# Four weight sums in DRAM moved out of the attention into the first merge pieces of a two-block layer

## The chip, the cores and the metric

The kernel runs on one core of a Trainium2 chip. The metric is the device time of one execution in microseconds. TensorE (PE in the profile) multiplies; VectorE (DVE) and ScalarE (ACT) work element by element; GpSimd (POOL) does little arithmetic here and issues the accumulating DMAs; SyncE (SP) issues nearly all the others.

## The reference, cut to what matters

Two transformer-like blocks run over 256 tokens of width 2048, in float32. The part that the change touches is in the second block, its projection, attention and merge, and the weights of its feed-forward part:

```python
proj = h @ w_in[i]                        # (256 x 2048) @ (2048 x 9216): u, v_sgu, q, k, v_att, g_a, g_b
z = einsum('bhqd,bhkd->bhqk', qi, kf) * scale
log_beta = log_sigmoid(z)
log_1m = where(strict, log_sigmoid(-z), 0)
tail = cumsum(log_1m, reverse=True) - log_1m
w = where(strict, exp(log_beta + tail), 0)
y_b = einsum('bhqk,bhkd->bhqd', w, vf)
merged = sigmoid(g_a) * (y_a @ w_up_a) + sigmoid(g_b) * (y_b @ w_up_b)
x = x + merged @ w_o
hid = rmsnorm(x) @ w_ffn_in
x = x + (silu(gate) * up) @ w_ffn_out
```

## The kernel before, in words

**Pieces.** All weights go through TensorE in 848 pieces of 256 rows by 512 columns (512 KB), numbered by `g`. Each piece passes four stages. SP loads it into the ring `raw` (8 slots, one load of 1 MB for two pieces). ACT copies it to `whi` in the format fp32r (`split_hi`), DVE subtracts to get the rest, `wlo` (`split_lo`, line 1874), and TensorE multiplies: eight matmuls with `whi` (line 1357), then four with `wlo` (line 1362), 512 columns each. `whi` and `wlo` have four slots (`RING`), so ACT and DVE can be at most four pieces ahead. ACT waits for TensorE to be done with the slot's last piece; SP waits for DVE (`lo_ready`) to be done with the slots that it fills.

**Order of the stages.** A (pieces 0 to 127), C, DP and D are the first block. E1 (pieces 196 to 275) is the projection of the second one, ten slabs of eight pieces, E2 (from piece 276, `g_plan`) the merge, G the output projection, F the feed-forward part, J the last gate. In E1 the attention is woven between the pieces, `w` counting them from 196: its two halves `b` begin at `ATT_START` = 35 and 55, which is piece 231 and piece 251. At `w = z0 + 5` DVE takes the scores (`att_take`), at `z0 + 6` and 7 ACT does Abs, Exp and Ln, at `z0 + 9` DVE makes the logs (`att_logs`: `Lp`, its mask, then `zt`), at `z0 + 10` TensorE does the tail matmuls (`att_tail`, lines 1622 to 1624, 12 in all), at `z0 + 14` DVE subtracts them (`att_arg`), and so on. At piece 235 TensorE also transposes the last keys (`tr2_slab`, line 1336); their banks are those that `att_take` frees. Ten `form_step`s at the pieces `FORM_AT` make sums of activations for the merge. After slab 4 of E1 SP issues `held` and `held_p` (2 MB and 0.5 MB from SBUF to DRAM).

**The merge.** Three groups of columns of the merge, and nine of the feed-forward part, are computed by a scheme with seven instead of eight products (pieces "s", half as many columns of work each: six matmuls, lines 1722 and 1726). It needs sums of weight tiles. Some of these are made beforehand in DRAM, in `summed[i]`, four for each group, group `c` reading number `4c` to `4c + 3`: SP copies one 1 MB term to `summed[i]` (line 670, `copies_for_sums`), and GpSimd adds the other with an accumulating DMA (line 881, `add_in_dram`). `SUM_AT[i]` is the piece at which this happens: SP issues the copy in front of the load of that piece, so some eight pieces ahead, after waiting for sum `i - 4`; GpSimd issues the add when TensorE has reached that piece. Between the adds GpSimd computes reciprocal roots (`POWS`), and `SUMS_UPTO` says up to which piece the sums stand in front of each. After them come the adds into `r1` for the merge groups (line 896).

**The plan of the loads.** From piece 276 on the loads come from a list, `PLAN.loads`, of (piece whose split frees the slot, piece that needs it, kind, ...), sorted by the first two. For the first merge group it holds, in this order: pair 280 (free at 269), pair 282 (271), pair 276 (273), pair 278 (275), pair 284 (277), pair 286 (279), halves 295 (280) and 296 (281), `r1` for 290 and 292 (282, two loads of 1 MB), halves 297 (282) and 298 (283), pair 288 (285), pair 294 (287). The load of `r1` for group 0 (`load_r1`, line 766 on) also waits until TensorE has done the first six pieces from 276 on (line 769) and for `ya2_ready`. `copies_for_sums(need)` is called in front of each.

Of the kernel before, what the change touches and what calls it, by code (L numbers as in the profile page):

```python
# [87 lines left out]
M_GROUPS = len(MERGE_S)  # L88
# [34 lines left out]
class Plan:  # L123
# [129 lines left out]
    def plan_s_loads(self, groups):  # L253

        n = self.halves
        for c in groups:
            at = lambda i: self.s_at[(c, *S_ORDER[i])]
            for h in range(2):
                free = {0: self.g_plan + 6, M_GROUPS: self.g_block}.get(c)
                free = self.s_at[c - 1, "M4", 2 * h + 1] if free is None else free  # L260
                self.loads.append((free, self.s_at[c, "M1", 2 * h], "r1", h, c))
                self.loads.append((self.s_at[c, "M1", 2 * h + 1], self.s_at[c, "M5", 2 * h], "fifth", h, c))
            for i, (m, q) in enumerate(S_ORDER):
                for what, first, last in (("b21", "M2", "M2"), ("b22", "M6", "M3"), ("seventh", "M7", "M7")):
                    if m == first:
                        slot = RAW // 2 + n % 4
                        need = at(i - S_LEAD if m == "M6" else i)
                        self.loads.append((self.last_use[slot], need, "half", slot, (c, what, q)))
                        self.half[c, what, q] = (slot, 16 * (n // 4 + 1))
                        self.last_use[slot] = self.s_at[c, last, q]  # L270
                        n += 1
        self.halves = n
# [42 lines left out]
def two_blocks_kernel(nc, A, out):  # L315
    PLAN = Plan()
# [3 lines left out]
    with ctx:  # L320
# [142 lines left out]

        summed = nc.dram_tensor("summed", (4 * S_GROUPS, P, 4 * COLS), F32, kind="Internal").ap()
        SUM_AT = [int(24 + SUM_STEP * i) for i in range(int(116 // SUM_STEP) + 1)] + [144 + 8 * i for i in range(7)]
        SUM_AT += [199 + int(5.4 * i) for i in range(14)]
        SUM_AT += [PLAN.g_out + 11 + 6 * i for i in range(4 * S_GROUPS - len(SUM_AT))]

        acc = ctx.enter_context(nc.psum_tensor("acc", [P, 4, COLS], F32))
# [352 lines left out]
        @block.gpsimd  # L822
        def _(pool):
            made = [0]

            def link(ins):
                made[0] += 1
                ins.then_inc(sem("pool_step"), 1)

            def settle():  # L830
                pool.wait_ge(sem("pool_step"), made[0])

            link(pool.memset(ident[:, :], 0.0))
            settle()
            link(pool.affine_select(out=ident[:, :], in_=ident[:, :], compare_op=ALU.not_equal, fill=1.0, base=0,
                                    pattern=[[-1, P]], channel_multiplier=1))
            settle()
            pool.sem_inc(sem("ident_ready"), 1)
            link(pool.memset(ones[:, :], 1.0))
            link(pool.memset(lmask[:, :, :, :], 1.0))  # L840
            link(pool.memset(flip[:, :], 0.0))
            link(pool.memset(sel[:, :, :], 0.0))
            settle()

            link(pool.affine_select(out=causal[:, :], in_=ones[:, 0:P], compare_op=ALU.is_ge, fill=0.0, base=0,
                                    pattern=[[1, P]], channel_multiplier=-1))
            link(pool.affine_select(out=strict[:, :], in_=ones[:, 0:P], compare_op=ALU.is_gt, fill=0.0, base=0,
                                    pattern=[[1, P]], channel_multiplier=-1))
            link(pool.affine_select(out=later[:, :], in_=ones[:, 0:P], compare_op=ALU.is_gt, fill=0.0, base=0,
                                    pattern=[[-1, P]], channel_multiplier=1))  # L850

            link(pool.affine_select(out=sel[:, :, :], in_=sel[:, :, :], compare_op=ALU.not_equal, fill=1.0, base=0,
                                    pattern=[[-1, 4], [0, P]], channel_multiplier=1))

            link(pool.affine_select(out=flip[:, :], in_=flip[:, :], compare_op=ALU.not_equal, fill=1.0, base=-(P - 1),
                                    pattern=[[1, P]], channel_multiplier=1))

            for n, s in enumerate(LEVELS[1:]):
                for t, (first, sign) in enumerate(((0, 1), (P - 1, -1))):
                    m = lmask[:, n, t, :].rearrange("p (n s) -> p n s", s=s)  # L860
                    link(pool.affine_select(out=m, in_=m, compare_op=ALU.is_ge, fill=0.0, base=first,
                                            pattern=[[-2 * s, 64 // s], [0, s]], channel_multiplier=sign))
            settle()
            for n, s in enumerate(LEVELS[1:]):
                for t, (first, sign) in enumerate(((0, 1), (P - 1, -1))):
                    m = lmask[:, n, t, :].rearrange("p (n s) -> p n s", s=s)
                    link(pool.affine_select(out=m, in_=m, compare_op=ALU.is_ge, fill=0.0, base=s - 1 - first,
                                            pattern=[[2 * s, 64 // s], [0, s]], channel_multiplier=-sign))
            link(pool.memset(minus_half[:, :], -0.5))
            settle()  # L870
            pool.sem_inc(sem("consts_ready"), 1)
            added = [0]

            def add_in_dram(upto):

                while added[0] < upto:
                    i = added[0]
                    added[0] += 1
                    pool.wait_ge(piece_used, SUM_AT[i])
                    pool.wait_ge(sem(f"copied{i % 4}"), 16 * (i // 4 + 1))  # L880
                    pool.dma_start(summed[i], sum_terms(i)[1], accum_op=ALU.add, max_dma_last_dim=8192)\
                        .then_inc(sem(f"summed{i % 4}"), 16)

            for i, (name, n) in enumerate(POWS):
                add_in_dram(len([g for g in SUM_AT if g <= SUMS_UPTO.get(name, 0)]))
                if name == "qk0":

                    pool.wait_ge(sem("ws_loaded"), 16)
                    pool.affine_select(out=wsT[:, :, :], in_=wsT[:, :, :], compare_op=ALU.is_ge, fill=0.0, base=0,
                                       pattern=[[0, 8], [1, P]], channel_multiplier=-1).then_inc(sem("ws_masked"), 1)  # L890
                if name in ("ffn", "ple"):
                    for c in range(M_GROUPS) if name == "ffn" else range(M_GROUPS, S_GROUPS):
                        for m, (what, before) in S_DMA.items():
                            for q in range(4):
                                pool.wait_ge(lo_ready, S_AT[c, before, q] + 1)
                                pool.dma_start(r1[:, q], s_weights(c, what, q), accum_op=ALU.add).then_inc(sem(f"r1_added{q}"), 16)
                if name == "ffn":
                    add_in_dram(len(SUM_AT))
                pool.wait_ge(pow_in, i + 1)
                pool.tensor_tensor(rstd[:, i, 0:n], var[:, i, 0:n], minus_half[:, 0:n], ALU.pow).then_inc(pow_out, 1)  # L900
# [961 lines left out]
        def _(dve):  # L1862
# [523 lines left out]
            def strict_blocks(x):  # L2386
                d = diagonal_blocks(x)
                return dve.tensor_tensor(d, d, strict[:, :].unsqueeze(1).unsqueeze(1).to_broadcast([P, 4, 2, P]), ALU.mult)

            def att_logs(b):  # L2390

                dve.wait_ge(sem("att_ln"), b + 1)
                link(dve.scalar_tensor_tensor(out=Lp[:, :, :], in0=zt[:, :, :], scalar=0.0, in1=ab[:, :, :], op0=ALU.max, op1=ALU.add))
                strict_blocks(Lp).then_inc(sem("att_l"), 1)
                link(dve.scalar_tensor_tensor(out=zt[:, :, :], in0=zt[:, :, :], scalar=0.0, in1=ab[:, :, :], op0=ALU.min,
                                              op1=ALU.subtract))

# [43 lines left out]
                        link(ins)  # L2441
                ins.then_inc(sem("ya2_ready"), 1)

            FORM_AT = [46, 47, 48, 50, 52, 54, 57, 58, 61, 65]

            def form_step(i):

# [16 lines left out]
            for s in range(10):  # L2464
                n = FIRST["E1"] + s
                for p in range(8):
# [49 lines left out]
                    for b, z0 in enumerate(ATT_START):  # L2516
                        if w == z0 + 5:
                            att_take(b)
                        if w == z0 + 9:
                            att_logs(b)  # L2520
                        if w == z0 + 14:
                            att_arg(b)
                        if w == z0 + 18:
                            att_mask(b)
                        if w == z0 + 21:
                            att_output(b)
# [317 lines left out]
```

## Time and profile before

| | us |
|---|---|
| median of 3 runs | 1904.59 |
| lowest and highest of them | 1903.56 and 1905.67 |
| the profiled execution | 1904.34 |
| its span (first to last instruction) | 1902.6 |
| TensorE busy (matmuls) | 1881.0 |
| VectorE busy | 1473.6 |
| ScalarE busy | 1141.5 |
| GpSimd busy | 129.6 |

The 16 DMA engines moved 535.95 MB, 282 GB/s on the mean. Matmul records are pipelined: one of 512 columns lasts 379 ns in the profile, but the next starts 216 ns after it. "PEclk" is the clock that TensorE was granted, 1.00 for 2.4 GHz; 0.50 is 1.2 GHz. In brackets stands the idle time of the engine before an instruction, and what ended it. The names `raw`, `ple` and `in_w_ffn_in` in the rows cover more than one tensor of the same place.

### The profile page before, as it was taken

Reading aid. Unit: us, or ns where it says so; the run is one execution under the profiler, and the core shown is the slowest. Engines: PE = TensorE matmul, PEld = TensorE weight load, DVE = VectorE, ACT = ScalarE, POOL = GpSimd, SP = SyncE. Lnnn points to the kernel's source line nnn. Section 1 sums busy time; section 2 is a strip of 40 time slices with the busy share of each in tenths; the row PEclk is TensorE's granted clock in tenths of the full one; section 3 lists DMA queues with packets and bytes.
Section 4 is the critical chain, followed back from the end, with each engine's and each line's share of the span. In section 5 each row is a group of like instructions: output and inputs, shape, how many; then the busy total and the mean of one; then the engine's idle time right before and its main releaser. Section 6 shows DMA issues by size and latency. Waiting matters only on the chain.

```text
span 1902.6 us, 23371 instructions
## 1 busy us (share of the span) xinstructions
PE 1881.0 (99%) x9018; PEld 1645.4 (86%) x9018; DVE 1473.6 (77%) x1591; ACT 1141.5 (60%) x1417; POOL 129.6 (7%) x156
## 2 busy tenths in 40 slices
PE   9999999999999989999999999999999999999998
PEld 8888888888888878888888888888888888888887
DVE  6889776655666757769899657989898999898865
ACT  7556445555565545656776555666766676666553
POOL 4000001000001100100000000000000000000000
PEclk9999999999999999999999999999999999999999
DMA  9799898999889999857987886798879887987653
GB/s 390 266 285 311 265 309 275 341 342 347 288 280 323 339 317 297 267 214 244 317 286 245 342 265 223 262 320 277 268 260 329 273 269 260 332 249 250 218 192 131
DMA packets 86815, 535.95 MB, mean 282 GB/s; under 512 B 10416, under 2 KB 11184, under 8 KB 40752
## 3 DMA queue, kind: packets, MB, share of 16 engines
q1 hardware_dynamic: 72736, 458.69, 63.3%
q0 software_dynamic: 13824, 75.50, 20.5%
q8 instruction: 72, 1.18, 0.2%
q10 hardware_dynamic: 144, 0.26, 0.0%
q14 instruction: 39, 0.32, 0.0%
HBM read 529.69 MB, written 105.38 MB: 334 GB/s over the span
## 4 chain that ended last, share of the span: by engine, by line
PE 86%; DVE 5%; DMA 4%; issue 3%; ACT 2%; POOL 1%; ACTq 0%; DVEq 0%; POOLq 0%
PE acc L1357 40%; PE acc L1362 20%; PE aux L1722 13%; PE aux L1726 7%; DMA raw<-in_w_in 2%; DVE wlo L1874 1%; PE aux L1336 1%; DVE wlo L2549 1%; ACT whi L926 1%; PE aux L1429 1%; DMA ple<-in_w_in 1%; DMA ple<-in_w_ffn_in 0%; PE aux L1803 0%; DVE ple L2544 0%; POOL rstd L900 0%
## 5 line engine op out<-in xcount | busy, mean ns | idle before, releaser
L1874 DVE TENSOR_TENSOR wlo<-raw,whi 128x1024 fp32r<-128x1024 f32 x512 | 624.0, 1226 | 313.9 <-ACT whi L926 306.7
L926 ACT ACTIVATE whi<-raw 128x1024 fp32r<-128x1024 f32 x511 | 533.9, 1054 | 466.4 <-PE acc L1362 413.1
L1357 PE MATMUL acc<-whi,actA_hi 128*128 128x512 f32 x892 | 344.1, 386 | 0.6 <-ACT whi L926 0.5
L1357 PE MATMUL acc<-whi,actA_lo 128*128 128x512 f32 x892 | 339.1, 380 | 0.0
L1357 PE MATMUL acc<-whi,actB_hi 128*128 128x512 f32 x796 | 305.1, 383 | 0.3 <-DVE actB_lo L2666 0.2
L1357 PE MATMUL acc<-whi,actB_lo 128*128 128x512 f32 x796 | 302.2, 380 | 0.0
L1175 ACT ACTIVATE whi<-ple 128x1024 fp32r<-128x1024 f32 x192 | 201.2, 1056 | 132.8 <-PE acc L1362 55.2
L2549 DVE TENSOR_TENSOR wlo<-ple,whi 128x1024 fp32r<-128x1024 f32 x192 | 230.8, 1221 | 27.7 <-ACT whi L1175 24.7
L1362 PE MATMUL acc<-wlo,actA_hi 128*128 128x512 f32 x892 | 228.9, 379 | 0.0
L1362 PE MATMUL acc<-wlo,actB_hi 128*128 128x512 f32 x796 | 205.5, 381 | 5.4 <-DVE wlo L1874 5.4
L2549 DVE TENSOR_TENSOR wlo<-raw,whi 128x1024 fp32r<-128x1024 f32 x144 | 174.4, 1221 | 25.5 <-ACT whi L1175 23.8
L1357 PEld LDWEIGHTS acc<-whi,actA_hi 128*128 128x128 f32 x892 | 169.1, 190 | 25.5 <-issue 2.0
L1362 PEld LDWEIGHTS acc<-wlo,actA_hi 128*128 128x128 f32 x892 | 168.8, 189 | 24.1
L1357 PEld LDWEIGHTS acc<-whi,actA_lo 128*128 128x128 f32 x892 | 169.3, 190 | 23.4 <-issue 0.5
L1175 ACT ACTIVATE whi<-raw 128x1024 fp32r<-128x1024 f32 x144 | 152.0, 1055 | 62.1 <-PE acc L1362 38.2
L1362 PEld LDWEIGHTS acc<-wlo,actB_hi 128*128 128x128 f32 x796 | 150.8, 190 | 27.6 <-DVE wlo L1874 6.2
L1357 PEld LDWEIGHTS acc<-whi,actB_hi 128*128 128x128 f32 x796 | 150.9, 190 | 22.2 <-DVE actB_lo L2666 1.0
L1357 PEld LDWEIGHTS acc<-whi,actB_lo 128*128 128x128 f32 x796 | 150.8, 190 | 20.8
L1722 PE MATMUL aux<-whi,actB_hi 128*128 128x512 f32 x360 | 136.8, 380 | 0.0
L1722 PE MATMUL aux<-whi,actB_lo 128*128 128x512 f32 x360 | 136.4, 379 | 0.0
L1726 PE MATMUL aux<-wlo,actB_hi 128*128 128x512 f32 x360 | 107.4, 380 | 0.7 <-DVE wlo L2549 0.7
L1722 PE MATMUL aux<-whi,actA_hi 128*128 128x512 f32 x216 | 82.9, 384 | 0.0
(366 smaller groups left out, 2381.8 us busy)
## 6 DMA issues: line engine op xcount, KB each, us to landing
raw<-in_w_in SPq DMA_DIRECT2D x108, 1024.0 KB, 7.6
raw<-in_w_ffn_out SPq DMA_DIRECT2D x44, 1024.0 KB, 6.9
summed<-in_w_ffn_in POOLq DMA_DIRECT2D x36, 1024.0 KB, 11.5
raw<-in_w_ffn_in SPq DMA_DIRECT2D x72, 512.0 KB, 7.8
ple<-summed SPq DMA_DIRECT2D x24, 1024.0 KB, 4.7
raw<-summed SPq DMA_DIRECT2D x48, 512.0 KB, 4.8
ple<-in_w_ffn_in SPq DMA_DIRECT2D x18, 1024.0 KB, 7.1
ple<-in_w_ffn_in POOLq DMA_DIRECT2D x36, 512.0 KB, 9.9
```

What stands on the lines that cost most here:

```text
L926: act.activation(whi[:, g % RING], raw_piece(g), ACT.Copy).then_inc(hi_ready, 1)
L1175: act.activation(whi[:, g % RING], s_source(c, m, q), ACT.Copy).then_inc(hi_ready, 1)
L1336: ins = pe.transpose(bank(u)[:, c * S + t * P:c * S + (t + 1) * P], src[:, t, (c0 + c) * P:(c0 + c + 1) * P], ident[:, :])
L1357: pe.matmul(acc2(n)[:, t, :], act[x][:, k + c, t * P:(t + 1) * P], woven(whi, g, c), start=(p == 0 and c == 0 and x == 0), stop=False)
L1362: ins = pe.matmul(acc2(n)[:, t, :], act[0][:, k + c, t * P:(t + 1) * P], woven(wlo, g, c), start=False, stop=(last and c == PK - 1))
L1429: ins = pe.matmul(bank(u)[:, c], Kp[n % 2][:, c], Qp[n % 2][:, c], start=True, stop=True)
L1722: pe.matmul(o, lhs(x, q * PK + k), woven(whi, g, k), start=(q == 0 and k == 0 and x == 0 and not onto), stop=False, skip_group_check=onto)
L1726: ins = pe.matmul(o, lhs(0, q * PK + k), woven(wlo, g, k), start=False, stop=(q == 3 and k == PK - 1), skip_group_check=onto)
L1874: dve.tensor_tensor(wlo[:, g % RING], raw_piece(g), whi[:, g % RING].bitcast(F32), ALU.subtract)\
L2549: dve.tensor_tensor(wlo[:, g % RING], s_source(c, m, q), whi[:, g % RING].bitcast(F32), ALU.subtract)\
```

## The change

Three things are moved. The sums: of the 14 from piece 199 on, those at 220, 226, 231 and 236 go, and four are put at pieces 277, 281, 285 and 289. The numbers `i` are given in order, so each sum from number 34 to 43 moves to another place; GpSimd adds the four in the branch that issues the adds into `r1`. The load of `r1` for merge group 0 takes piece 285 in place of 282 as the one that frees it, which puts it behind halves 297 and 298 and pair 288 in the sorted list. The last step of `att_logs`, on `zt`, becomes `att_negative` and runs one piece later, and the last `form_step` two pieces later.

```diff
@@ plan_s_loads
-                free = {0: self.g_plan + 6, M_GROUPS: self.g_block}.get(c)
+                free = {0: self.g_plan + 9, M_GROUPS: self.g_block}.get(c)
@@ two_blocks_kernel
-        SUM_AT += [199 + int(5.4 * i) for i in range(14)]
+        SUM_AT += [199 + int(5.4 * i) for i in (0, 1, 2, 3, 8, 9, 10, 11, 12, 13)]
+        SUM_AT += [PLAN.g_plan + 1 + 4 * i for i in range(4)]
@@ gpsimd
                     for c in range(M_GROUPS) if name == "ffn" else range(M_GROUPS, S_GROUPS):
+                        add_in_dram(len([g for g in SUM_AT if g < S_AT[c, "M6", 0]]))
@@ vector
                 strict_blocks(Lp).then_inc(sem("att_l"), 1)
+
+            def att_negative(b):
+
                 link(dve.scalar_tensor_tensor(out=zt[:, :, :], in0=zt[:, :, :], scalar=0.0, in1=ab[:, :, :], op0=ALU.min,
                                               op1=ALU.subtract))
@@
-            FORM_AT = [46, 47, 48, 50, 52, 54, 57, 58, 61, 65]
+            FORM_AT = [46, 47, 48, 50, 52, 54, 57, 58, 61, 67]
@@
                         if w == z0 + 9:
                             att_logs(b)
+                        if w == z0 + 10:
+                            att_negative(b)
```

## Rows read from the trace of the kernel before

**Rows 1.** Order of time, TensorE alone, lines 1362: both attention blocks.
```profile
684.14 1.03 PE L1362 MATMUL acc<-wlo,actB_hi 128*128 128x512 f32 x4
...
704.18 1.03 PE L1362 MATMUL acc<-wlo,actB_hi 128*128 128x512 f32 x4
710.64 2.08 PE L1362 MATMUL acc<-wlo,actB_hi 128*128 128x512 f32 x4 [3.71 <-DVE wlo L1874]
719.68 1.03 PE L1362 MATMUL acc<-wlo,actB_hi 128*128 128x512 f32 x4
722.27 1.03 PE L1362 MATMUL acc<-wlo,actB_hi 128*128 128x512 f32 x4
...
771.60 1.03 PE L1362 MATMUL acc<-wlo,actB_hi 128*128 128x512 f32 x4
776.06 1.13 PE L1362 MATMUL acc<-wlo,actB_hi 128*128 128x512 f32 x4 [1.71 <-DVE wlo L1874]
...
782.27 1.03 PE L1362 MATMUL acc<-wlo,actB_hi 128*128 128x512 f32 x4
```

**Rows 2.** Chain that ended last, 716 to 740 us: start, us, what.
```profile
736.25 0.89 PE aux L1636 x8
```

**Rows 3.** Chain that ended last, 645 to 692 us.
```profile
658.35 27.83 DMA raw<-in_w_in
```

**Rows 4.** Order of time, all engines, 680 to 735 us.
```profile
686.20 2.00 ACT L926 ACTIVATE whi<-raw 128x1024 fp32r<-128x1024 f32 x2 [12.86 <-DMA raw<-in_w_in]
...
689.12 1.91 PE L1336 MATMUL aux<-ident,gate 128*128 128x128 f32 x8 [3.96 <-DVE att_z L2381]
...
707.58 1.75 DVE L2395 SCALAR_TENSOR_TENSOR att_z<-att_z,att_ab 128x1536 f32<-128x1536 f32 x1
```

**Rows 5.** Windows of 5 us: busy time by engine, PEclk, DMA share, GB/s.
```profile
690.00:695.00 5.00, 5.00 (x21) 4.34 (x20) 1.60 (x2) 4.35 (x4) 0.00 (x0) 0.74 0.93 252
...
710.00:715.00 5.00, 4.36 (x12) 3.71 (x13) 4.97 (x5) 1.06 (x1) 0.81 (x1) 0.50 0.76 228
...
775.00:780.00 5.00, 3.94 (x24) 3.65 (x25) 4.85 (x5) 3.89 (x16) 0.00 (x0) 1.00 0.60 202
```

**Rows 6.** Order of time, VectorE, second attention block.
```profile
773.00 1.75 DVE L2395 SCALAR_TENSOR_TENSOR att_z<-att_z,att_ab 128x1536 f32<-128x1536 f32 x1
```

**Rows 7.** DMA queues of the page: packets, MB, share of 16 engines' span.
```profile
q1 hardware_dynamic: 72736, 458.69, 63.3%
q0 software_dynamic: 13824, 75.50, 20.5%
```

**Rows 8.** Windows of the stretches around and behind the attention.
```profile
600.00:655.00 55.00, 54.92 (x263) 47.92 (x263) 37.55 (x39) 29.72 (x69) 10.26 (x6) 1.00 1.02 329
...
790.00:810.00 20.00, 20.00 (x106) 17.84 (x106) 13.25 (x18) 9.56 (x10) 0.81 (x1) 1.00 0.83 243
810.00:860.00 50.00, 50.00 (x249) 44.10 (x248) 30.93 (x44) 29.12 (x40) 0.00 (x0) 1.00 0.58 211
860.00:905.00 45.00, 45.00 (x210) 39.26 (x209) 42.09 (x38) 30.92 (x32) 3.52 (x4) 1.00 0.80 257
```

**Rows 9.** Source line 680, the 11 weight loads issued from 600 to 656 us.
```profile
DMA to landing us min/median/max: 7.8/14.1/16.2
```

**Rows 10.** Source line 762, the 6 weight loads issued from 790 to 840 us.
```profile
DMA to landing us min/median/max: 4.6/4.8/6.9
```

**Rows 11.** Order of time, SyncE's issues, 650 to 660 us.
```profile
655.51 0.44 SPq L736 DMA_DIRECT2D held_resid<-resid  x1
...
656.98 0.50 SPq L670 DMA_DIRECT2D summed<-in_w_ffn_in  x1
```

**Rows 12.** Waits of SyncE, 800 to 860 us: us, times, longest.
```profile
SPq L769 <- PE acc L1362: 10.1, 1, 10.1
```

**Rows 13.** Order of time, SyncE's issues, 820 to 850 us.
```profile
844.58 0.33 SPq L762 DMA_DIRECT2D raw<-in_w_in  x1
```

**Rows 14.** Order of time, ScalarE, 850 to 858 us.
```profile
855.42 2.00 ACT L926 ACTIVATE whi<-raw 128x1024 fp32r<-128x1024 f32 x2 [4.04 <-DMA raw<-in_w_in]
```

## Prediction, made before the changed kernel was run

> **What bounds the kernel now.** I read the page first, then five-microsecond windows over the whole span, then the order of time where TensorE was idle. TensorE is the bound: it is idle for 21.6 of 1902.6 us, so a change can gain only where it stands still or runs at its lower clock. In the stretches that the change touches there are two such places, both in the attention of the second block (pieces 231 to 272).
>
> The last four matmuls of every eight-chunk piece (line 1362) are a good clock. Undisturbed, a piece takes 722.27 - 719.68 = 2.59 us. From piece 235 (684.14) to piece 242 (719.68) pass 35.54 us [rows 1]. Work there: seven pieces, 18.13; eight transposes, 0.89 [rows 2]; the tail matmuls of the first attention block, which in the second block take 782.27 - 776.06 - 2.59 = 3.62, of which 0.10 is the restart of the group before, so 3.52. Together 22.54; **lost 13.0 us**. It falls in two parts: up to 704.18 pass 20.04 for 13.84 of work (6.2 lost), after it 15.50 for 8.70 (6.8 lost). In the second attention block 4.46 us pass between pieces 260 and 261, with 2.59 of work: **1.9 lost**. In all 14.9 us.
>
> What each loss is:
> - Loss one (6.2). The load of piece 236 is issued at 658.35 and takes 27.83 us [rows 3]; ACT's split waits 12.86 us for it. DVE takes the attention scores only behind its own half of that split, and TensorE's transposes need the banks which that frees: 3.96 us idle [rows 4]. The rest is clock: 0.74 of full in the window behind the gap [rows 5], so part of it at 1.2 GHz, and a short wait at 699.
> - Loss two (6.8). DVE, still late, does the three steps of att_logs in one go; the last one, `zt`, takes 1.75 us [rows 4]. The low half of piece 241 comes after it and TensorE waits 3.71 us [rows 1]. Again the clock falls, to 0.50 in 710 to 715 [rows 5], and the tail matmuls run at 1.2 GHz.
> - Loss three (1.9). The same burst in the second block, with no late load before it: 1.71 us idle behind a `zt` step of 1.75 [rows 1, 6]; there the clock stays at 2.4 GHz, 1.00 granted [rows 5].
>
> **The change, part by part.**
>
> *Four sums leave the attention.* Sums at pieces 220, 226, 231 and 236 go; those from 242 on stay where they are, with other data. One sum is a 1 MB DRAM-to-DRAM copy on SP's queue and a 1 MB accumulating DMA on GpSimd's. The engine time of the latter is 20.5% of 1902.6 us for 75.5 MB, 5.2 us per MB; SP's queue takes 63.3% for 458.69 MB, 2.6 us per MB [rows 7]. No row separates copies from loads; a copy also writes DRAM, so it costs 2.6 (the mean) to 5.2 (an add, which reads twice and writes), and I take 2.8. A sum is then 8.4 us of all 16 engines for 1.05 MB and four are 34 us (bounds 33 to 44). From 600 to 655 the DMA share is 1.02 [rows 8], so this is work on a full resource: loads land after 14.1 us (median) there [rows 9] against 4.8 in the merge [rows 10]. Directly in front of the late load stand 2.6 MB of held data (residual and `p_2`), issued from 655.51 on, and the copy for piece 236 at 656.98 [rows 11]; the adds for 220, 226 and 231 run around it. After the change what is left in front is one load and the held data, 4.7 MB with the load itself: 12 us at 2.6, 25 at 5.2; I take 14, for the SP queue has no copy and GpSimd's no add to share with. Issued at 656.5 the load lands near 670 (668 to 681). ACT stopped for it at 686.20 - 12.86 = 673.3 [rows 4], and TensorE at 689.12 - 3.96 = 685.2, and from landing to TensorE's start went 689.12 - 686.20 = 2.9 us; so only a landing after 682 would stop it. So loss one goes: -6.2, even at the pessimistic end, and with it DVE's lateness.
>
> *The `zt` step one piece later.* It costs the same 1.75 us plus 0.03 of link, but the low half of piece 241 (and 261) comes first. In the second block the wait was 1.71, the step 1.78: nothing is left of it, with no margin (-1.9, bounds -1.4 and -1.9). In the first block, once the load is in time, the case is that of the second block with a 1.4 us scaling where the other has 1.22: about the same zero margin. I leave 0.3 us of idle over both, and take -6.8 for loss two; short idle like this left the clock up in loss three. Behind the moved step wait the split of piece 242 and form step 0; TensorE has the 3.5 us of tail matmuls there, which cover 1.78. If DVE were still late this would be 2 us of idle again. The last form step goes from 65 to 67 to make room (one subtraction-sized step, in place of which stands the `zt` step); it is wanted only after piece 285, so 0.
>
> *Four sums into the merge.* Their copies are issued ahead of the loads for pieces 280, 282, 286 and 295, between about 793 and 828; the adds follow TensorE at pieces 277, 281, 285 and 289, some 2.6 us a piece, from about 825 to 861 on the old clock. SP spends 0.5 us more on each, 2.0 in all, and waits for nothing (each copy needs the sum four before it: for 289 that of 269, eleven pieces or 28 us older when SP gets there). GpSimd has nothing between these adds and those into r1, 20 pieces on. The DMA's idle time is 17% of 20, 42% of 50 and 20% of 45 us: 33.4 us [rows 8], against 34 (33 to 44) added: on the mean it just about fits until 905. What covers it is that TensorE never waits there today, busy for 50.00 of 50.00 and 45.00 of 45.00 us [rows 8], and that the DMA's idle time stands before the load-heavy pieces, not behind them. If that cover is gone a load is late at a piece of the first merge group. Cost 0, bounds 0 and 7 (first rival).
> The Trainium skill (DMA: Bandwidth & Descriptors, "Queues, rings and completion order") says that each DMA engine takes turns, packet by packet, between the queues that have work. By it a merge load beside an add gets half the engines' turns, and 4.8 us become up to 10; that speaks against this move, and the case it gives is the first rival. The 14.1 against 4.8 us agree with it in direction.
>
> *The r1 load three pieces later.* Now SP waits 10.1 us for TensorE at its line 769 [rows 12], then issues r1, two halves and, at 844.58, the pair for piece 288 [rows 13]; ACT then waits 4.04 us for that pair [rows 14]. After the change halves and pair go first and r1 (2 MB) at about 845. The pair lands some 4 us sooner; r1's first half is wanted by ACT when the splits of 288 and 289 are done, at 857.4 today. Issue plus 14.1, the median under full load, is 859, 1.7 later, but ACT and DVE then have the 4 us in hand that the earlier pair gives. So 0 gained (TensorE is busy through there), 0 lost, with a thin margin.
>
> **Sum.** The profiled execution took 1904.3 us (span 1902.6). 1904.3 - 6.2 - 6.8 - 1.9 + 0.3 = 1889.7; the median of the runs is 0.3 above it: **1890.0 us**.
>
> **Rivals.**
> 1. *A wait in the merge replaces part of the gain.* For: DMA filled to the brim in 800 to 905, r1 issued late, and pieces of half length from 290 on, which take 512 KB in 1.3 us. Against: TensorE never waits there now. Price: one load that takes 9.6 us, midway between 4.8 and the 14.1 of the full stretch, so 4.8 late, less what ACT and DVE have in hand (I take 2), costs 3 us of idle and, as in loss two, about as much again by the clock: +7, **1897**. Chance 0.15.
> 2. *The load of piece 236 stays late*, because the 2.6 MB of held data in front of it, and not the sums, make it so: they stand in the same queue and stay. Then loss one stays, and of loss two only the `zt` step goes (1.8 of 6.8, its clock share kept); with loss three 3.7 gained: **1901**. Chance 0.07.
> 3. *The burst is not cured*: the loads come in time, but DVE stays late at 241 and 261 by 1 to 2 us. **1892 to 1893**. Chance 0.07.
> 4. *Slower.* The merge becomes bound by DMA: the 34 us added are not covered by the gaps, because the loads there are issued just in time, and pile up as TensorE waits at pieces 288 to 330. It decides once more than 14.6 of them are on the path; with all 34, 1890 + 34 = **1924**. Against: 42% of 810 to 860 is free. Chance 0.03. The Trainium skill (DMA: Bandwidth & Descriptors, "Bandwidth") gives 425 GB/s for a core alone; an estimate by it: 27 MB now in 790 to 905 and 8.4 MB more are 308 GB/s, far from that bound, so the page sides against this rival.
> 5. *It does nothing*, both waits coming back elsewhere in the attention: 1904. Chance 0.02.
> My forecast has the remaining 0.66.
>
> **How the numbers follow.** A measurement of this kernel can tell 0.2%, 3.8 us, from no change. The forecast, rivals 1 and 3 and half of rival 2, which lies on the border, are faster by more: 0.92. The other half and rival 5 give 0.05 within it; rival 4 gives 0.03 slower. All three losses gone is the floor: 1890.0 less the 0.3 left over, less a run's scatter of 1.1, less 0.6 for errors of the differences between rows: low end 1888.0. The upper end takes in rivals 3 and 1: 1897.5.
>
> **What the changed profile would show.** The load of piece 236 landing within about 15 us, ACT's wait for it gone, TensorE busy at 5.00 in every window and PEclk 1.00 throughout the attention; `zt` behind the low half of the next piece; DMA share near 1.0 from 800 to 870 with adds in it. It would be wrong if r1 lands more than 15 us after its issue, if a TensorE idle of over 3 us with a fallen clock stands at pieces 288 to 330, or if DVE has lost more than 2 us by piece 241.

## The result and the profile after

| | before, us | changed, us |
|---|---|---|
| median | 1905.13 (6 runs, 1902.46 to 1908.90) | 1893.01 (6 runs, 1892.05 to 1893.44) |
| span of the profiled execution | 1902.6 | 1891.3 |
| TensorE busy | 1881.0 | 1877.2 |

The ratio is 0.9936, 95% interval 0.9923 to 0.9949: 0.64% faster, 12.1 us where 14.6 were forecast. The time lies inside the range, 3.0 us above the point. The gain is far outside what the measurement is uncertain by. Lines of the changed kernel stand one or two further down than in the kernel before (670 became 671, 1362 became 1364), five or seven further behind `att_negative`.

**The attention.** Order of time, TensorE alone, of the changed kernel, the same `wlo` groups as in [rows 1]:

```profile
684.36 1.03 PE L1364 MATMUL acc<-wlo,actB_hi 128*128 128x512 f32 x4
...
687.83 1.03 PE L1364 MATMUL acc<-wlo,actB_hi 128*128 128x512 f32 x4
...
698.19 1.03 PE L1364 MATMUL acc<-wlo,actB_hi 128*128 128x512 f32 x4
700.78 1.03 PE L1364 MATMUL acc<-wlo,actB_hi 128*128 128x512 f32 x4
...
706.88 1.03 PE L1364 MATMUL acc<-wlo,actB_hi 128*128 128x512 f32 x4
...
758.80 1.03 PE L1364 MATMUL acc<-wlo,actB_hi 128*128 128x512 f32 x4
761.47 1.13 PE L1364 MATMUL acc<-wlo,actB_hi 128*128 128x512 f32 x4
...
767.67 1.03 PE L1364 MATMUL acc<-wlo,actB_hi 128*128 128x512 f32 x4
```

From piece 235 to 242 now pass 706.88 - 684.36 = 22.52 us, where the prediction counted 22.54 of work: nothing of the 13.0 lost us is left. Between pieces 260 and 261 pass 2.67 us with 2.59 of work. No bracket is left either: TensorE waits for nothing in this stretch.

Order of time, SyncE, 650 to 660 us, and ScalarE from 675 us: the copy that stood at 656.98 [rows 11] is gone, and the split of piece 236, which waited 12.86 us for its load [rows 4], now waits for TensorE to free the slot, as it should:

```profile
655.72 0.43 SPq L737 DMA_DIRECT2D held_resid<-resid  x1
656.20 0.47 SPq L739 DMA_DIRECT2D held_p<-p1T_hi  x1
656.71 0.88 SPq L739 DMA_DIRECT2D held_p<-p1T_lo  x1
658.43 0.33 SPq L681 DMA_DIRECT2D raw<-in_w_in  x1
```

```profile
677.71 1.06 ACT L928 ACTIVATE whi<-raw 128x1024 fp32r<-128x1024 f32 x1 [4.15 <-PE acc L1364]
```

The load landed 12.6 us after its issue, at 671.0 (27.83 before, [rows 3]). Order of time, VectorE: the low half of piece 241 stands in front of the `zt` step and is through at 700.33, 0.45 us before TensorE wants it at 700.78.

```profile
697.97 1.23 DVE L2390 TENSOR_TENSOR att_l<-att_l,strict 128x1024 f32<-128x1024 f32 x1
699.11 1.22 DVE L1876 TENSOR_TENSOR wlo<-raw,whi 128x1024 fp32r<-128x1024 f32 x1
700.25 1.75 DVE L2400 SCALAR_TENSOR_TENSOR att_z<-att_z,att_ab 128x1536 f32<-128x1536 f32 x1
```

**Piece by piece.** Each piece ends with an increment of one semaphore, whose times the trace holds. The difference of these times between two executions shows where one is ahead. The changed kernel starts the attention 0.2 us behind, and is ahead of the one before by 5.6 us at piece 236, 6.0 at 239, 10.9 at 241, 12.8 at 242, 14.6 from 261 to 299: 14.8 gained in the attention. Then it gives back: 1.6 us at pieces 300 to 302, 1.2 at 323, 0.3 at 361. At piece 400 it is ahead by 11.6 and at the end by 11.3.

**The merge.** The waits of TensorE over the stretch 600 to 960 us of the changed kernel (us, times, longest), its windows, and ScalarE at pieces 300 to 303:

```profile
PE aux L1724 <- ACT whi L1177: 1.4, 2, 0.8
PE acc L1359 <- ACT whi L928: 0.2, 1, 0.2
```

```profile
600.00:655.00 55.00, 54.92 (x263) 47.68 (x262) 37.34 (x39) 30.65 (x69) 9.44 (x5) 1.00 0.88 283
655.00:690.00 35.00, 35.00 (x176) 30.90 (x175) 19.33 (x22) 20.43 (x31) 2.54 (x1) 1.00 0.78 286
...
776.00:796.00 20.00, 20.00 (x106) 17.86 (x105) 13.84 (x18) 8.96 (x10) 0.81 (x1) 1.00 1.03 326
796.00:846.00 50.00, 50.00 (x249) 44.08 (x249) 34.21 (x47) 29.23 (x40) 2.46 (x4) 1.00 0.95 312
846.00:906.00 60.00, 58.00 (x263) 48.94 (x262) 47.34 (x43) 39.09 (x42) 4.31 (x5) 1.00 0.91 303
```

```profile
863.26 1.06 ACT L1177 ACTIVATE whi<-raw 128x1024 fp32r<-128x1024 f32 x1 [4.64 <-DMA raw<-summed]
864.50 2.27 ACT L1177 ACTIVATE whi<-raw 128x1024 fp32r<-128x1024 f32 x2 [0.18 <-DMA raw<-summed]
866.96 1.06 ACT L1177 ACTIVATE whi<-raw 128x1024 fp32r<-128x1024 f32 x1 [0.19 <-DMA raw<-summed]
```

The DMA share before the late load fell from 1.02 [rows 8] to 0.88 and 0.78; that of the merge, which was 0.83, 0.58 and 0.80, rose to 1.03, 0.95 and 0.91. The four half-piece loads of sums for pieces 300 to 303 are issued when their slot comes free and are wanted about 5 us later. Landing times from source line 788, 853 to 859 us, after, and from its counterpart 787 before, 868 to 874 us:

```profile
DMA to landing us min/median/max: 8.5/9.8/9.9
```

```profile
DMA to landing us min/median/max: 4.8/5.4/6.1
```

Of the 1.4 us in the first of these rows, 0.66 stand at piece 300 and 0.79 at piece 323; the 1.6 us given back at pieces 300 to 302 are the former and matmuls stretched behind it. DVE, late by then, releases the fourth add into `r1` 7.1 us after piece 310 and not 6.2 as before; that add is what piece 323 waits for. The granted clock stays at 1.00 in all of these windows.

One of the prediction's signs of being wrong did come. Landing times of the two halves of `r1`, issued at 830.44 and 830.9 us:

```profile
DMA to landing us min/median/max: 9.3/12.8/16.4
```

The second half took more than 15 us, and ACT waited 3.05 us for it; TensorE did not.

### The profile page after: what moved, and what is told of

It reads as the page before. It is cut to its first block, busy times and chain, and to the rows that moved or that the text cites. A ratio compares the mean times of both kernels' runs of the same rounds, so it can differ in the third digit from the quotient of the medians.

```text
span 1891.3 us, 23371 instructions
## 1 busy us (share of the span) xinstructions
PE 1877.2 (99%) x9018; PEld 1641.9 (87%) x9018; DVE 1471.8 (78%) x1591; ACT 1140.8 (60%) x1417; POOL 130.4 (7%) x156
## 4 chain that ended last, share of the span: by engine, by line
PE 90%; DVE 5%; DMA 3%; issue 1%; ACT 1%; POOL 0%; SPq 0%; ACTq 0%; DVEq 0%; POOLq 0%
PE acc L1359 44%; PE acc L1364 22%; PE aux L1724 12%; PE aux L1728 6%; DVE wlo L2556 2%; PE aux L1338 2%; DMA ple<-in_w_ffn_in 1%; DVE wlo L1876 1%; PE aux L1431 1%; DVE ple L2551 1%; DMA ple<-in_w_in 1%; DMA raw<-summed 1%; PE aux L1805 0%; ACT whi L928 0%; ACT whi L1177 0%
## 6 DMA issues: line engine op xcount, KB each, us to landing
summed<-in_w_ffn_in POOLq DMA_DIRECT2D x36, 1024.0 KB, 11.6
```

## The experiments

Ten kernels, and twice the changed kernel again, in three groups; the kernels of a group share a chip and the runs of the kernel before. The profiled executions differ by up to 2.8 us before the attention begins (mostly 1.6 to 1.7 us at piece 70, or at piece 88, that are lost or not), so for effects of a few us I go by the differences piece by piece within a stretch, and by the ratio for the whole.

### Each part by itself

`e1_zt_only`, the kernel before with:

```diff
-            FORM_AT = [46, 47, 48, 50, 52, 54, 57, 58, 61, 65]
+            FORM_AT = [46, 47, 48, 50, 52, 54, 57, 58, 61, 67]
...
+                        if w == z0 + 10:
+                            att_negative(b)
```

> The kernel before with only the `zt` step one piece later and the last form step two pieces later; sums and r1 as before. If the late load of piece 236 is what makes loss one, it stays whole (6.2 us), loss three goes (1.9) and of loss two only 1.8: 1905.1 - 3.7 = 1901.4 us, ratio 0.998. Rival: the burst of att_logs alone makes loss two, so all of 6.8 goes: 1905.1 - 8.7 = 1896.4 us.

Measured: 1898.96 us beside 1903.55, ratio 0.9978 (0.9968 to 0.9988), about 4.2 us. Waits of TensorE, 660 to 880 us:

```profile
PE acc L1362 <- DVE wlo L1874: 1.9, 1, 1.9
PE acc L1357 <- ACT whi L926: 1.9, 3, 0.9
PE aux L1336 <- DVE att_z L2381: 1.1, 1, 1.1
PE aux L1726 <- DVE wlo L2554: 0.6, 1, 0.6
```

The wait behind the `zt` step went from 3.71 to 1.9, by the step's own 1.78, and loss three went (1.8 at piece 261). ACT still waits 10.0 us for one weight load, so loss one is not the burst's. How late that load is against TensorE differs between executions: in this one the wait of the transposes was 1.1 and not 3.96. The theory's 3.7 us holds, the rival's 8.7 does not.

`e2_sums_only`, the kernel before with the sums of the diff and the `add_in_dram` in GpSimd's branch, and nothing else:

> The kernel before with only the four sums moved; `zt` in att_logs and r1 at its old place. Theory: the load of piece 236 lands within 15 us, loss one goes (6.2); at piece 241 DVE has 0.63 us in hand in the changed kernel and needs 1.78 more here, so 1.2 us of idle stay of loss two's 6.8, without a fallen clock; loss three stays whole (1.9). 3 us or more come back in the merge. 1905.1 - 6.2 - 5.6 + 3.1 = 1896.4 us. Rival (the held data make the load late): loss one stays, time about 1905.

Measured: 1905.06 us beside 1903.55, ratio 1.0006 (0.9997 to 1.0014): **no gain at all**. In the attention it did what was expected: ahead by 5.8 us at piece 236, and by 0.4, 3.4 and 1.9 more at 239, 241 and 242, so that 1.5 of loss two and loss three stay. But 8.4 us come back in one place, at piece 288:

```profile
PE acc L1359 <- ACT whi L928: 5.8, 1, 5.8
PE acc L1364 <- DVE wlo L1876: 3.0, 2, 1.7
```

```profile
852.75 2.00 ACT L928 ACTIVATE whi<-raw 128x1024 fp32r<-128x1024 f32 x2 [10.91 <-DMA raw<-in_w_in]
```

A miss: the theory said 1896.4, with 3.1 us coming back in the merge, and nothing on record named this load as the one that would be late. It is the wait of 4.04 us of [rows 14] grown to 10.91, past the slack that ACT and DVE have.

`e3_r1_early`, the changed kernel with the first line of the diff undone:

```diff
-                free = {0: self.g_plan + 9, M_GROUPS: self.g_block}.get(c)
+                free = {0: self.g_plan + 6, M_GROUPS: self.g_block}.get(c)
```

> The changed kernel with the r1 load back at its old place (free at 282). Theory A (the merge gives back 3.1 us because four sums fill the DMA engines): the r1 order matters little for pieces 300 to 323, the waits there stay, and one is added at pieces 288 to 292, because the pair for 288 is again behind r1: 1893 to 1896 us. Theory B (the late r1 pushes the loads behind it and so makes the waits at 300 and 323): they go, 1890 us.

Measured: 1902.14 us beside 1903.55, ratio 0.9995 (0.9986 to 1.0004), a miss for both theories. Order of time, TensorE, 835 to 870 us, and the windows of 5 us around it:

```profile
851.26 0.77 PE L1359 MATMUL acc<-whi,actB_hi 128*128 128x512 f32 x1 [6.18 <-ACT whi L928]
```

```profile
845.00:850.00 5.00, 0.08 (x1) 0.00 (x0) 0.00 (x0) 0.00 (x0) 0.00 (x0) 0.88 1.02 301
850.00:855.00 5.00, 3.74 (x9) 3.05 (x10) 3.85 (x4) 3.90 (x4) 0.00 (x0) 0.50 0.20 82
855.00:860.00 5.00, 5.00 (x24) 4.30 (x23) 4.86 (x5) 2.11 (x2) 0.82 (x1) 0.94 0.89 264
```

So the order of one load is worth 8.6 us in the changed kernel: 6.2 of idle and 2.4 of TensorE at 1.2 GHz behind it. The mechanism is the queue: SP waits at `r1`'s condition, then issues 2 MB of `r1` and two halves, and only then the pair for piece 288, which is wanted first. That pair landed 18.1 us after its issue here; in the changed kernel, where it stands in front of `r1`, 7.3. It does not settle what makes the waits at pieces 300 and 323. Both are gone here, as theory B said. The last add follows TensorE and so came later too, at 856.54 and not 845.97; but it landed after 8.4 us and not 11.8, for the DMA engines had emptied while TensorE stood (0.20 in 850 to 855), and the halves for pieces 300 to 303 took 5.8 to 7.3 us and not 8.5 to 9.9. Whether the stall or the early `r1` emptied them cannot be told from this run. The late `r1` alone does not make the waits, for with it late and the sums light (below) there are none; that the sums would make them with `r1` early and no stall is not shown.

`e8_r1_late_only`, the kernel before with that one line changed to `+ 9`:

> The kernel before with only the r1 load three pieces later. Theory: without the sums in the merge TensorE waits for nothing at pieces 288 to 292 in either order, so the reordering is worth nothing by itself, ratio 1.000; its 8 to 9 us in the changed kernel come only with the four sums in the queues. Rival: it gains or costs 2 us or more by itself.

Measured: 1902.67 us beside 1905.25, ratio 0.9991 (0.9981 to 1.0001), no difference that can be told. Between pieces 242 and 400 the distance between the two executions changes by 0.2 us, so the reordering by itself gives nothing in the merge.

In the attention, which this edit does not touch, this execution is 5.0 us faster than the profiled one of the kernel before. Its late load kept ACT waiting 10.7 us and not 12.86, and behind the same wait of 3.71 us at piece 241 the clock did not fall:

```profile
705.00:710.00 5.00, 1.40 (x7) 0.89 (x5) 4.93 (x5) 0.82 (x1) 0.00 (x0) 1.00 0.36 156
710.00:715.00 5.00, 4.89 (x30) 4.55 (x31) 4.93 (x6) 1.06 (x1) 0.81 (x1) 1.00 0.82 251
```

In the kernel before 710 to 715 was at 0.50 [rows 5]; in `e1_zt_only` a wait of 1.9 us at piece 241 was followed by 0.70. So the three losses, 14.8 us in one execution, are 9.8 in another, and the length of the one wait does not say whether the clock falls.

The three parts do not add up: `zt` alone 0.22%, sums alone nothing, `r1` alone nothing that can be told, all three 0.64%. Sums and `r1` without `zt` were not run.

### What fills the merge

`e4_light_sums`, the changed kernel with the DMAs of the four sums in the merge cut to 1/32 and group 10 reading group 9's sums (`e5_light_adds` has the second edit alone). Both leave out work of the reference, so their results are not the reference's:

```diff
-                    sp.dma_start(summed[i], sum_terms(i)[0]).then_inc(sem(f"copied{i % 4}"), 16)
+                    n = 64 if 40 <= i < 44 else 4 * COLS
+                    sp.dma_start(summed[i][:, 0:n], sum_terms(i)[0][:, 0:n]).then_inc(sem(f"copied{i % 4}"), 16)
...
-                    pool.dma_start(summed[i], sum_terms(i)[1], accum_op=ALU.add, max_dma_last_dim=8192)\
+                    n = 64 if 40 <= i < 44 else 4 * COLS
+                    pool.dma_start(summed[i][:, 0:n], sum_terms(i)[1][:, 0:n], accum_op=ALU.add, max_dma_last_dim=8192)\
```

> The changed kernel in which the four sums numbered 40 to 43, made at pieces 277, 281, 285 and 289, are cut to 64 of 2048 columns, copy and add; feed-forward group 10 reads the sums of group 9 in their place. Theory A: with some 34 us of DMA time taken out of 776 to 860 us the halves for pieces 300 to 303 land in 5 to 6 us and not in 10, the waits at pieces 300 and 323 go but for the 0.25 us that the kernel before has at 323: 1893.0 - 2.8 = 1890.2 us. Theory B: they stay, 1893 us.

> The changed kernel in which only the adds of the four sums 40 to 43 are cut to 64 of 2048 columns, so these sums lack their second term; their copies stay whole. If the adds are what fills the DMA engines (5.2 us of all 16 each, against 2.6 to 5.2 for a copy) most of the 2.8 us given back in the merge goes: 1890 to 1891 us. If copies in SP's own queue, in front of the loads, do it, 1892 to 1893 us.

Measured: 1891.75 us beside 1903.55, ratio 0.9941 (0.9928 to 0.9953), midway between the two theories, and 1890.82 beside 1905.25, ratio 0.9924 (0.9911 to 0.9937), the latter with the changed kernel itself, `c0_changed`, beside it:

> The changed kernel itself once more, as the measure for the three runs beside it: 12 us under the kernel before, ratio 0.9936.

That one gave 1893.46, ratio 0.9934 (0.9921 to 0.9947). The pieces decide more sharply than the medians. Between pieces 261 and 400 the changed kernel gave back 3.0, 2.5 and 2.9 us in its three profiled executions; with light sums 0.2, with light adds and whole copies 0.2. So the waits need the DMA load of the four sums, and nearly all of it is the adds: cutting them alone takes away as much as cutting both.

The packets in the trace say why. The copies of the sums are the only packets of 64 KB: 768 of them in the kernel before, 50.33 MB, took 2.35 us of all 16 engines per MB. The adds into DRAM, also 50.33 MB, took 5.0, and loads in packets of 8 KB took 2.6. So an add takes 5.2 us of all 16 engines and a copy 2.5, and the four copies had landed by 820.2 us, 33 us before the first of the late loads was issued. While an add moves its packets there are about as many load packets as add packets, 11 to 20 beside 16 to 22 per us from 850 to 857 us in the changed kernel. But one of an add takes 656 ns and one of a load 342, so the loads are down to about a third: some 130 KB per us beside an add, 400 to 450 without.

### Where the sums could go

`e6_sums_ffn`: all four out of the merge, the last ones in the first feed-forward pieces.

```diff
-        SUM_AT += [PLAN.g_plan + 1 + 4 * i for i in range(4)]
-        SUM_AT += [PLAN.g_out + 11 + 6 * i for i in range(4 * S_GROUPS - len(SUM_AT))]
+        SUM_AT += [PLAN.g_out + 11 + 6 * i for i in range(4)]
+        SUM_AT += [PLAN.g_ffn + 3 + 8 * i for i in range(4 * S_GROUPS - len(SUM_AT))]
...
-                    add_in_dram(len(SUM_AT))
+                    add_in_dram(len([g for g in SUM_AT if g < PLAN.g_ffn]))
```

> The changed kernel with the four sums out of the merge as well: four sums at pieces 419 to 437 as before, the last four at 443, 451, 459 and 467, in the first feed-forward pieces, where the DMA share is 0.56 to 0.85. The result is the reference's. Theory: the merge gives nothing back and the feed-forward part has room: 2.8 us under the changed kernel, 1890.2 us. Rival: the DMA engines are as full there when the first feed-forward group comes, and 1 to 3 us come back at pieces 458 to 491: 1891 to 1893 us.

Measured: 1904.97 us beside 1905.25, ratio 0.9998 (0.9990 to 1.0007). A miss, for theory and rival. The merge gives nothing back, as said, but 13.1 us are lost at one place, piece 468:

```profile
1212.67 0.77 PE L1724 MATMUL aux<-whi,actB_hi 128*128 128x512 f32 x1 [11.54 <-ACT whi L1177]
```

```profile
1165.00:1200.00 35.00, 35.00 (x168) 30.67 (x167) 26.45 (x25) 19.57 (x20) 2.44 (x3) 1.00 0.94 317
1200.00:1215.00 15.00, 3.46 (x12) 2.56 (x11) 2.44 (x3) 3.17 (x3) 0.00 (x0) 0.71 1.03 354
```

The changed kernel has DMA shares of 0.78 and 0.63 in the same stretches, and I had read such shares as room. The loads of half pieces come in bunches there; with a copy in SP's queue and two adds beside them, each took 19.0 to 21.2 us instead of 3.7 to 6.0.

Then three versions that keep the sums among full pieces, with the changed kernel beside them:

> The changed kernel again, as the measure on this chip: ratio 0.9935.

It gave 1893.94 us, ratio 0.9943 (0.9929 to 0.9956).

`e10_three_and_one`, the last sum at 443 instead of 289:

```diff
-        SUM_AT += [PLAN.g_plan + 1 + 4 * i for i in range(4)]
+        SUM_AT += [PLAN.g_plan + 1 + 4 * i for i in range(3)]
```

> The changed kernel with only the last sum, the one at 289, taken out of the merge and made at 443 instead. The result is the reference's. If the wait at piece 300 comes from the adds of 285 and 289 together, about half of the 2.8 us comes back, 1891.5 us; if the add of 289 alone, running from 846 to 858 us, makes it, all: 1890.2 us.

Measured: 1890.90 us, ratio 0.9925 (0.9912 to 0.9939), 3.0 us under the changed kernel. The wait at 300 is gone whole, and that at 323 but for 0.2 us. TensorE's waits, 600 to 960 us:

```profile
PE acc L1359 <- ACT whi L928: 0.2, 1, 0.2
```

Taking out the last sum alone is enough.

`e7_two_back`, with `(0, 1, 2, 3, 4, 5, 8, ...)` in the attention and `range(2)` in the merge:

> The changed kernel with two of the four sums back in the attention, at pieces 220 and 226; the merge keeps two, at 277 and 281. The result is the reference's. Theory: what made the load of piece 236 late were mainly the copies for 231 and 236, in SP's queue right in front of it, and the adds beside it; with these gone it still lands before 682 us and all 14.6 us of the attention stay; the adds of 277 and 281 have landed by 836 us, so the halves for 300 land in time: 1893.0 - 2.8 = 1890.2 us. Rival: two sums are enough to make that load late: 3 to 10 us slower than the changed kernel.

Measured: 1890.74 us, ratio 0.9925 (0.9912 to 0.9939), 3.2 us under the changed kernel. The load of piece 236, issued at 658.57:

```profile
DMA to landing us min/median/max: 17.6/17.6/17.6
```

It landed 1.7 us before TensorE freed the slot for ACT's split; the attention is as fast as in the changed kernel. So without the sums at 231 and 236 the load is in time, though those at 220 and 226 and the held data are still there. In the kernel before, the add for 231 was issued at 674.28 and that for 236 at 685.47, 0.7 us before the load landed; so of these two sums only the copies and the first add can have delayed it. An estimate from the prices above: two copies at 2.5 us and an add at 5.2 are 10.2 us, and the load took 27.8 with them and 17.6 without. The 5.0 us between 17.6 and the changed kernel's 12.6 are about one more add, that for 226. In the merge 0.9 us is still given back, 0.8 of it at piece 323, where the fourth add into `r1` took 11.2 us to land and not 10.4.

`e9_one_two_one`, with one sum back at 220, `range(2)` in the merge, and so a fifth at the output projection:

```diff
-        SUM_AT += [199 + int(5.4 * i) for i in (0, 1, 2, 3, 8, 9, 10, 11, 12, 13)]
-        SUM_AT += [PLAN.g_plan + 1 + 4 * i for i in range(4)]
+        SUM_AT += [199 + int(5.4 * i) for i in (0, 1, 2, 3, 4, 8, 9, 10, 11, 12, 13)]
+        SUM_AT += [PLAN.g_plan + 1 + 4 * i for i in range(2)]
```

> The changed kernel with one sum back at piece 220, two in the merge at 277 and 281, and five instead of four at the output projection, 419 to 443, all among full-size pieces. The result is the reference's. Theory: full-size pieces take 512 KB in 2.59 us, half-size ones in 1.30, so only among the former is there room for a sum; no wait is left at 300 or 323, and none comes at 458 to 480: 1890.2 us. Rival: the fifth sum, whose add lands 7 pieces before the first feed-forward group, makes a wait there of 1 to 13 us.

Measured: 1889.02 us (4 runs, 1888.89 to 1889.96), ratio 0.9916 (0.9902 to 0.9930): **the fastest version**, 4.9 us under the changed kernel beside it, whose fastest run was 1893.41. The theory had 1890.2; the rival's wait did not come. Pieces 261 to 400 give back 0.2 us where the changed kernel beside it gives back 2.9; of the rest, most lies behind piece 500, and its cause was not looked for. That full-size pieces are the only ones with room is not shown by it: `e7_two_back` and `e10_three_and_one` come within 2 us.

## Why the prediction was right, and where it was off

- **What bounds the kernel.** Right. The three losses were measured as the changed kernel removed them: loss one 6.2 (5.8 at piece 236, 0.4 at 239) for 6.2; loss two 6.8 (4.9 and 1.9) for 6.8; loss three 1.8 for 1.9. Together 14.8 us against 14.6, the forecast's 14.9 less 0.3. That the forecast met the medians rests on a typical execution having been read: `e8_r1_late_only`, with the same attention, lost only 9.8.
- **"Four sums leave the attention."** Right in the mechanism. The load landed at 671.0 where 670 was said, by two errors that cancel: it was issued at 658.4 and not 656.5, and took 12.6 us and not 14. The copies for 231 and 236 and the add for 231 made it late (`e7_two_back`); rival 2 is excluded by that. Rival 3 did not come either. A copy was put at 2.6 to 5.2 us per MB and taken as 2.8; the packets show 2.35, so four sums are 31 us of all 16 engines and not 34.
- **"The `zt` step one piece later."** Right. By itself it took away 1.8 us of loss two's wait and loss three (`e1_zt_only`). That a short idle leaves the clock up, said there of 0.3 us, was not tried: no idle was left.
- **"Four sums into the merge", cost 0.** This is the term that was mis-sized: it measured 2.5 to 3.0 us. The mechanism was that of rival 1, at the half pieces and by loads that took 9.8 us, as its price assumed. Its price of 7 (3 of idle and as much again are 6) counted a fallen clock; behind the waits of 0.66 and 0.79 us the clock stayed at 1.00. The step's argument, that the idle DMA time before piece 290 covers the added work on the mean, did not see that the last add (piece 289) runs right before and into the bunch of loads for piece 300; moving that one sum was enough. The rule of the Trainium skill (DMA: Bandwidth & Descriptors, "Queues, rings and completion order") on turns between queues, set beside it, pointed the right way: loads beside an add took 8.5 to 9.9 us, where by half the turns 4.8 would become up to 10. The trace agrees with the turns, about one packet for one. It does not agree with the step from there to half the rate, for an add's packet takes nearly twice as long as a load's; these loads took no more than 10 us because the add's packets end at 858, with loads back at 400 KB per us and more.
- **"The r1 load three pieces later", "0 gained".** Right only for the kernel before (`e8_r1_late_only`). In the changed kernel it is worth 8.6 us (`e3_r1_early`), and without it the sums bring nothing (`e2_sums_only`). I priced the edit against the profile of before and not against the queues that the other edit makes. The sum came out near all the same, because both were made together and I had taken the wait at 288 as covered with the new order. That is in part luck: nothing in the prediction says that without this edit the other would gain nothing.
- **Rivals 4 and 5.** Neither came. The data rate at which rival 4 was found far from its bound says little here: the engines were 91 to 103% busy from 776 to 906 us at 303 to 326 GB/s, because adds hold them twice as long per byte.
- **The forecast as a whole.** 14.6 less the 2.5 to 3.0 given back is 11.6 to 12.1; the two sets of six runs give 12.1. The point was 3.0 us too low, for this one term. The low end of the range, 1888.0, held even for `e9_one_two_one`, which has neither the three losses nor the waits in the merge and took 1889.0.

## What to carry to other kernels

Price a moved transfer at the place where it lands in the queue: which load is issued next behind it, how long after its issue that load is wanted, and whether a reordering in the same change is what keeps it in time; such edits have no price one by one. Background traffic belongs among the stages that need few bytes per us of TensorE, and its last piece must have landed before a bunch of just-in-time loads begins: a mean DMA share of 0.6 to 0.8 over a stretch of bunches is no room. Read the packets of each kind apart before pricing a transfer: here an add cost twice a copy. A late load is paid for more than once, here by idle, in some executions by the lower clock after it, and by an engine that then has no slack for its next burst.

## What I had not expected of the hardware

- Two adds beside half-piece loads, and a copy in front of them, stretched each of these from 3.7 to 6.0 us to 19.0 to 21.2, and cost 13.1 us at a single piece (`e6_sums_ffn`); a mean share of 0.94 stood in the 35 us before it.
- Cutting only the adds freed as much as cutting adds and copies (0.2 us given back in both), though a copy moves the same 1 MB and stands in the loads' own queue. Per MB a copy from DRAM to DRAM took 2.35 us of all 16 engines, less than a load (2.6), and an add into DRAM 5.0. Copies issued at the time of the late loads, and not between 774 and 811 us, were not tried.
- The kernel before scatters more than the changed one: its runs in these sessions lie between 1899.5 and 1909.1 us, those of the changed kernel between 1891.8 and 1895.1. Its late load differs from execution to execution (ACT waited 12.86, 10.7 and 10.0 us for it in three profiles with the same queues), and so does the clock behind it (0.50 or 1.00 after the same wait of 3.71 us), which fits; that this is the whole of the scatter was not shown.
